# Wide token-major projections and a first unit moved forward, in a hybrid decoder block on one core

## The reference

```python
mg = h @ w_in[:, gate columns]                            # 2 x 1024 columns, "mg"
b_ssm = y_ssm @ w_branch_ssm                              # "bs"
b_nsa = o_nsa @ w_branch_nsa                              # "bn"
merged = sigmoid(mg[:, :1024]) * b_ssm + sigmoid(mg[:, 1024:]) * b_nsa
x = x + merged @ w_out                                    # "wo"
a = clamped_swiglu(t @ w_gate_up[e] + b_gate_up[e])       # per expert e
out = out + combine[:, e:e + 1] * (a @ w_down[e] + b_down[e])
```

## Time and profile before

| | |
|---|---|
| runs | 1303.49 median, 1302.44 to 1305.95 (n = 3) |
| profiled execution | 1304.99 us, span 1303.3 |
| granted clock, mean | 0.992 |
| PE busy | 1222.0 us, 94% of the span |
| DVE, ACT, POOL busy | 444.3, 281.1, 105.4 us |
| DMA | 454.08 MB, mean 348 GB/s |
| chain that ended last | PE 58%, DMA 31%, DVE 6%, ACT 3% |
| its largest lines | weights of w_gate_up 28%, PE L1032 20%, PE L1046 10%, PE L749 5% |

### The profile page before, as it was taken

How to read it: one execution, slowest core, us unless ns; L and a number is a source line. 1 busy time by engine, 2 the same in 40 slices (tenths; PEclk the granted TensorE clock), 3 DMA queues, 4 the chain that set the end, 5 groups by cost and what they waited for, 6 DMA issues and landing times.

```text
span 1303.3 us, 17482 instructions
## 1 busy us (share of the span) xinstructions
PE 1222.0 (94%) x7089; PEld 654.2 (50%) x7089; DVE 444.3 (34%) x914; ACT 281.1 (22%) x507; POOL 105.4 (8%) x89
## 2 busy tenths in 40 slices
PE   6999998999889999999999989898989999898985
PEld 6999987899853343343333324232323323242321
DVE  6866566665533222222122212122122212122113
ACT  4673437662321000110011101010101101010101
POOL 1301301453500000000000000000000000000000
PEclk9989999999989999999999999999999999999999
DMA  7647433225989999999999999999999999999994
GB/s 225 210 129 227 130 103 124 98 98 161 367 351 367 426 428 428 428 428 430 428 428 428 430 427 428 428 430 427 428 428 429 428 427 429 429 428 428 427 428 210
DMA packets 79964, 454.08 MB, mean 348 GB/s; under 512 B 10160, under 2 KB 53296, under 8 KB 55344
## 3 DMA queue, kind: packets, MB, share of 16 engines
q1 hardware_dynamic: 76960, 451.30, 84.8%
q10 hardware_dynamic: 2960, 2.17, 0.6%
HBM read 452.40 MB, written 1.05 MB: 348 GB/s over the span
## 4 chain that ended last, share of the span: by engine, by line
PE 58%; DMA 31%; DVE 6%; ACT 3%; issue 1%; ACTq 1%; POOL 0%; DVEq 0%; SPq 0%
DMA ring<-in_w_gate_up_dram 28%; PE psum L1032 20%; PE psum L1046 10%; PE psum L746 9%; PE psum L749 5%; PE psum L1021 5%; PE psum L1072 3%; DMA ring<-in_w_down_dram 3%; PE psum L700 2%; DVE WL L1461 2%; ACT WH L1173 1%; PE psum L956 1%; PE psum L1003 1%; PE psum L827 1%; DMA PR<-in_cmp_pos_v_dram 1%
## 5 line engine op out<-in xcount | busy, mean ns | idle before, releaser
L1032 PE MATMUL psum<-ring,ZS 128*64 128x512 f32 x1504 | 355.3, 616 | 13.6 <-DMA ring<-in_w_gate_up_dram 13.5
L1032 PEld LDWEIGHTS psum<-ring,ZS 128*64 128x64 f32 x1504 | 100.0, 134 | 229.7 <-issue 192.4
L1894 DVE TENSOR_TENSOR X<-X,psum 128x1024 f32<-128x1024 f32 x64 | 75.3, 1218 | 387.8 <-PE psum L1072 387.8
L1046 PE MATMUL psum<-ring,HT 128*64 128x512 f32 x784 | 176.3, 596 | 20.4 <-DMA ring<-in_w_down_dram 19.7
L1878 DVE TENSOR_SCALAR ZS<-psum 128x512 f32<-128x512 f32 x32 | 22.1, 692 | 316.3 <-PE psum L1032 316.3
L1032 PE MATMUL psum<-slot,ZS 128*64 128x512 f32 x528 | 123.8, 615 | 2.0 <-DMA slot<-in_w_gate_up_dram 2.0
L1046 PEld LDWEIGHTS psum<-ring,HT 128*64 128x64 f32 x784 | 54.5, 136 | 129.6 <-issue 104.6
L1461 DVE TENSOR_TENSOR WL<-ring,WH 128x2048 fp32r<-128x2048 f32 (+1 forms) x42 | 98.4, 2344 | 56.7 <-ACT WH L1173 56.7
L1380 ACT ACTIVATE HT<-psum 128x512 f32<-128x512 f32 x32 | 19.1, 597 | 324.3 <-PE psum L700 324.3
L1173 ACT ACTIVATE WH<-ring 128x2048 fp32r<-128x2048 f32 (+1 forms) x42 | 78.5, 1874 | 13.1 <-PE psum L749 9.3
L1032 PEld LDWEIGHTS psum<-slot,ZS 128*64 128x64 f32 x528 | 35.7, 134 | 73.3 <-issue 64.6
(11 more groups left out here) (321 smaller groups left out, 1230.1 us busy)
## 6 DMA issues: line engine op xcount, KB each, us to landing
ring<-in_w_gate_up_dram SPq DMA_DIRECT2D x94, 2048.0 KB, 33.8
ring<-in_w_down_dram SPq DMA_DIRECT2D x49, 2048.0 KB, 35.1
slot<-in_w_gate_up_dram SPq DMA_DIRECT2D x33, 2048.0 KB, 33.8
ring<-in_w_in_dram SPq DMA_DIRECT2D x30, 1024.0 KB, 5.5
slot<-in_w_down_dram SPq DMA_DIRECT2D x15, 2048.0 KB, 35.0
ring<-in_w_branch_ssm_dram SPq DMA_DIRECT2D x4, 1024.0 KB, 4.9
ring<-in_w_branch_nsa_dram SPq DMA_DIRECT2D x4, 1024.0 KB, 4.9
ring<-in_w_out_dram SPq DMA_DIRECT2D x4, 1024.0 KB, 4.9
```

What stands on the lines that cost most here:

```text
L1032: ins = mm(psum[64 * (c % 2):64 * (c % 2) + 64, c // 2, :], XTS[:, k, s], every_other_pair(w[:, 2048 * (k % 2):2048 * (k % 2) + 2048], c), ...
L1046: ins = mm(psum[64 * h:64 * h + 64, 2, :], lhs, w[:, at:at + 512], start=(j + hf + k == 0), stop=(j == 1 and hf + k == 2))
L1894: v.tensor_tensor(xo, xo, psum[:, 3 + 2 * t:5 + 2 * t, :], ALU.add).then_inc(o_read, 1)
```

## The change

Units of mg, bs, bn and the first two of wo are cut the other way: 512 rows of weights by 512 columns. Two neighbouring units make a pair: the even one does the first half of the contraction, the odd one the second, into the same banks. A pair holds two banks, one per token half, and is evicted after its odd unit: t = 0 at H, t = 1 at P. A half of a unit is 3 passes of 4 matmuls with 512 columns. bn's halves wait only for the PV results that they read, so bn 0 and bn 1 join the list of fillers; the steps 0, 1 and 2 take two halves each. W now stands ahead of its H. MT and the first XX work by token half (four blocks of one t) rather than by column pairs. wo 2 and wo 3 stay as they were.

```diff
@@ order of the tokens
-    for x in [("mg", m) for m in range(2, 8)] + [("bs", m) for m in range(4)]:
+    for x in [("mg", m) for m in range(2, 8)] + [("bs", m) for m in range(4)] + [("bn", 0), ("bn", 1)]:
         halves += [("H", u[x]), ("P", u[x])]
...
         out.append(halves.pop(0))
+        if k < 3:
+            out.append(halves.pop(0))
...
     out += halves + [("LD", 0)]
-    for m in range(4):
-        unit("bn", m)
-        if m >= 1:
-            out.append(("MT", m - 1))
-    out.append(("MT", 3))
...
+    for m, behind_h, behind_p in ((2, [("MT", 0)], [("MT", 1)]), (3, [], [])):
+        out += [("H", u[("bn", m)]), *behind_h, ("P", u[("bn", m)]), *behind_p]
+    out += [("H", u[("wo", 0)]), ("MT", 2), ("P", u[("wo", 0)]), ("MT", 3)]
+    out += [("H", u[("wo", 1)]), ("P", u[("wo", 1)]), ("XX", 0)]
+    out += [("H", u[("wo", 2)]), ("RM", 0), ("XX", 1), ("P", u[("wo", 2)]), ("RM", 1)]
+    out += [("H", u[("wo", 3)]), ("XX", 2), ("P", u[("wo", 3)]), ("RM", 2)]
@@ loads on SP
+                    if wide(u):
+                        rows = slice(512 * (m % 2), 512 * (m % 2) + 512)
+                        c0 = first.get(kind, 0) + 512 * (m // 2)
+                        sp.dma_start(slot_view(u, 4, 512), w[0, rows, c0:c0 + 512].rearrange("(k p) n -> p k n", p=P)
+                                     ).then_inc(full, 16)
@@ PE
+            def wide_half_unit(u, t):
+                kind, m = UNITS[u]
+                h = m % 2
+                b, before = bank_of[u][t], freed[u][t]
+                if h == 0:
+                    pe.wait_ge(proj_free[b], before)
+                if kind == "bs" and m == 0 and t == 0:
+                    pe.wait_ge(ys_ready, 1)
+                if kind == "bn":
+                    pe.wait_ge(pv_read, 8 * t + 4 * h + 4)
+                if kind == "wo":
+                    pe.wait_ge(mt_ready, 2 * h + t + 1)
...
+                for n, (w, src) in enumerate([(wh, high), (wh, low), (wl, high)]):
...
+                    if n == 1 and kind == "wo":
+                        pe.wait_ge(mt_low, 2 * h + t + 1)
+                    for k in range(4):
+                        ins = mm(bank(b, 512), src[:, 4 * h + k, P * t:P * t + P], w[:, k, :],
+                                 start=(h == 0 and n == 0 and k == 0), stop=(h == 1 and n == 2 and k == 3))
+                if t == 1:
+                    ins.then_inc(unit_done, 1)
+                elif h == 1:
+                    ins.then_inc(wide_half, 1)
@@ DVE, eviction of bn
+                        ga = GA[:, t, D + 512 * q:D + 512 * q + 512]
+                        v.scalar_tensor_tensor(out=ga, in0=ga, scalar=1.0, in1=psum[:, b],
+                                               op0=ALU.add, op1=ALU.mult).then_inc(proj_free[b], 1)
+                        dve.wait_ge(proj_free[b], freed[k][t] + 1)
+                        v.tensor_tensor(MG[:, t, cols], MG[:, t, cols], ga, ALU.add).then_inc(mg_ready, 1)
```

More of the change, by code:

```diff
@@ L76, with wide @@
 SPLIT_UNITS = [u for u, (kind, _) in enumerate(UNITS) if kind not in ("w1k", "w1v")]
+def wide(u):
+    kind, m = UNITS[u]
+    return kind in ("mg", "bs", "bn") or (kind == "wo" and m < 2)
+PAIRS = [u for u in range(NU) if wide(u) and UNITS[u][1] % 2]
 def token_order():
@@ L165, in token_order @@
                 low.append(("L", SPLIT_UNITS[i]))
+        order.append(token)
+        if token[0] == "RW":
+            order += low
+            low = []
         if not first <= n < last:
@@ L392, in hybrid_block @@
                 continue
-            bank_of[u], freed[u] = n % 3, uses[n % 3]
-            uses[n % 3] += 1
-            n += 1
+            if wide(u) and UNITS[u][1] % 2:
+                bank_of[u], freed[u] = bank_of[u - 1], freed[u - 1]
+                continue
+            took = []
+            for _ in range(T if wide(u) else 1):
+                took.append((n % 3, uses[n % 3]))
+                uses[n % 3] += 1
+                n += 1
+            bank_of[u], freed[u] = zip(*took) if wide(u) else took[0]
         def slot_view(u, *dims):
@@ L712, in _ @@
             pe.wait_ge(const_done, 2)
+            def wide_half_unit(u, t):
+                kind, m = UNITS[u]
+                h = m % 2
[8 more added lines that the diff above has]
+                    pe.wait_ge(mt_ready, 2 * h + t + 1)
+                high, low = {"bs": (YSH, YSL), "bn": (OTH, OTL), "wo": (HTH, MTL)}.get(kind, (HTH, HTL))
+                i = SPLIT_UNITS.index(u)
+                wh, wl = part(WH[i % SPLITS], 0, 4, 512), part(WL[i % SPLITS], 0, 4, 512)
+                if t == 0:
+                    pe.wait_ge(wh_ready, i + 1)
+                for n, (w, src) in enumerate([(wh, high), (wh, low), (wl, high)]):
+                    if w is wl and t == 0:
+                        low_ready(pe, i)
+                    if n == 1 and kind == "wo":
[7 more added lines that the diff above has]
+                    ins.then_inc(wide_half, 1)
             def half_unit(u, half):
                 kind, m = UNITS[u]
+                if wide(u):
+                    return wide_half_unit(u, half)
                 b = bank_of[u]
@@ L720, in half_unit @@
                         pe.wait_ge(proj_free[b], freed[u])
[L721 to L724, removed]
                 feature_major = kind in ("xbc", "kc", "vc", "ks", "kw", "q", "z")
-                high, low = {"bs": (YSH, YSL), "bn": (OTH, OTL), "wo": (HTH, MTL)}.get(kind, (HTH, HTL))
+                high, low = (HTH, MTL) if kind == "wo" else (HTH, HTL)
                 rows = slice(P * half, P * half + P)
@@ L964, in _ @@
                         pe.wait_ge(mt_low, k - 1)
[L965 to L968 removed]
+                    q, t = k // 2, k % 2
+                    for j in range(4):
+                        ins = tr(bank(3 + k % 2, 4, P)[:, j], MG[:, t, P * (4 * q + j):P * (4 * q + j) + P])
                     ins.then_inc(mt_full, 1)
@@ L982, in _ @@
                     pe.wait_ge(h2t_act, k + 1)
-                    for t in range(T):
-                        router(k, t)
+                    if k < 2:
+                        for m in range(2):
+                            router(m, k)
+                    else:
+                        for t in range(T):
+                            router(2, t)
             for t in range(T):
```

137 lines of the change are left out of this document (76 added, 61 removed).

## The result

The changed kernel takes **1289.79 us** (median of four runs, 1288.22 to 1291.53) against 1302.97 (four runs, 1301.91 to 1305.95) of the kernel before on the same chip: a ratio of 0.9898, 95% interval 0.9881 to 0.9915, or 13.2 us faster. The prediction was 1288.3, inside 1282 to 1296. Two later sets of runs of the same kernel, each on its own chip, gave 1290.24 and 1289.70, with 1304.60 and 1304.35 for the kernel before beside them: 14.4 and 14.7 us between the medians, 13.7 and 13.4 by the ratios.

The account below looks back on a forecast made before the run. The expert weight stream was taken as the bound, its end set by the dense stage's end: 1304.99 less 15.2 gives 1289.8, and the median 1.5 below that 1288.3, range 1282 to 1296 us.

Parts of the forecast that it names:

- The last unit: Last half unit before the expert part: ends 15.2 us earlier than 363.47, at 348.3.
- Width: Half units: 512-column matmuls at 218 ns, bounds 213 and 248; a half takes 2.7 us with re-entry instead of 2.98.
- Steps 0 to 4: Early attention: three more half units done, PT5 at 240.0 instead of 237.74, so 2.3 us later.
- Steps 5 to 16: Later attention: ACT/DVE loop at 12.1 us per two steps; 0.8 gained where PE was bound; PV15 ends at 304.1.
- The tail to wo 1: PV15 to wo1's end: ten halves, four transpose groups, 1.4 us wait on DVE; ends 333.7, 15.6 earlier.
- The clock: Tail: the 0.73 granted clock behind the 3.71 us pause cost 1.6 us; the share should now be near one.
- The weights: Expert loads: shift 12.4 (first two), 10.5 (third), 13 (fourth), 15 to 16 us (others); stream ends 15.2 earlier.
- (a): Whole dense stage: PE is the only bound, contention mild; 19 to 21 us earlier, 1284; chance 0.17.
- (b): Tail: DVE low parts at 4.23 beside POOL and the clock falls again; 10 us earlier, 1293.5; chance 0.13.
- (c): Expert weight stream: queue full from the third load, so only its 10.5 us shift counts; 1293; chance 0.06.
- (d): Split-format 512-column matmul takes about 427 ns, decisive from 274; some 66 us slower, 1370; chance 0.03.
- (e): No difference: moved halves push the loop by the tail's saving, halves no shorter (248 ns), PV15 at 312 or later; chance 0.03.

Follow-up runs that it names:

- The experiment on the width: Changed kernel with every 512-column matmul split into two of 256 columns: 1293.12 us, 2.9 above the changed kernel on the same chip.
- the order experiment: Changed kernel with MT 2 and MT 3 both ahead of wo 0's halves: 1296.25 us, 6.0 above the changed kernel.
- the experiment with the third load: Changed kernel with the third expert load issued behind wo 0 instead of behind bn 3: 1291.03 us, 0.8 above the changed kernel on the same chip.
- the kernel with nothing moved: Changed kernel with wide units and reordered tail kept, but no half unit moved into the attention: 1296.10 us, 5.9 above the changed kernel.

## Why the prediction was right, and where its terms were not

**The whole.** Mechanism and size held: a forecast gain of 15.2 us, 13.3 in the trace's stretch, 13.2 in the medians (14.4 and 14.7 on the two other chips). That the profiled executions differ by 15.9 is no confirmation, since 2.0 of it are ahead of the change. The last unit was to end 167.4 us behind the start of the stretch (348.3 less 180.92) and ended at 169.24, 1.9 late. Of that, 0.7 had come by the end of PV(15) and 1.2 came in the tail up to wo 1. The terms, all counted from that start:

- **Width.** I took 218 ns from the nearest row, 215 ns; it is 227, 213 for the columns and 13.5 more. With bounds of 213 and 248 it is inside, and a half unit is 2.72 back to back, and 2.86 behind anything else, where I had 2.62 and 2.7. This is the mis-sized term; of the signs that the prediction named, the spacing of 215 to 220 ns and the last unit at 348 (350.2 in the same count) are the ones that did not come. The rule quoted in the prediction (the Trainium skill, "TensorE: Matmul & The Clock Gate", section Back-to-back issue gap, about 131 ns) is contradicted by the operation itself now.
- **Steps 0 to 4.** The times came nearly to the tenth: the bank of mg 4's second half at 33.67 (33.6 forecast), PT(2) at 44.13 (44.0), PT(4) at 53.82 (54.0), the SSM output's low part at 56.37 (56.3), PT(5) at 59.14 (59.1), with the wait on VectorE's copy that the forecast named. But two errors cancel here, which is luck. Between 33.67 and 53.82 five half units took 14.2 us (2.90, 5.58, 2.87, 2.86) where 13.5 were forecast, and three groups of transposes, PV and scores took 1.98 each where 2.3 were forecast. The timeline of before has 2.01 for such a group, from PT(1) at 214.90 to the half unit at 216.91.
- **Steps 5 to 16.** From PT(5) to the end of PV(15) 64.1 were forecast and 64.75 came. Before it was 64.87, so the 0.8 us that this part was to gain came to 0.1: the six steps from PT(9) to PT(15) gained 0.66 (34.73 against 35.39), and the steps from PT(5) to PT(9) took 0.54 back (23.03 against 22.49). The mechanism was only half right: I had the ACT and DVE loop as the bound at 12.1 us for two steps; the steps run at 2 x 6.13 = 12.26 with no listed wait of PE behind 261.09 and up to 301, so PE is the bound, with the loop just behind. The experiment on the width shows both: the pitch follows PE's width to 6.25, in full from PT(9) on, and still only 1.3 of some 3.4 us of width count in all up to PV(15).
- **The tail to wo 1.** Forecast 29.6, measured 30.81. Four groups of transposes took 1.4 (1.6 forecast) and the wait 1.19 (1.4). Ten halves with their re-entries took 28.2, not 26.6: 1.0 for the width (27.2 at 2.72 each where 26.2 were forecast) and 0.6 for the re-entries, which cost 1.0, not 0.4. The wait was right by two errors that cancel. ScalarE was not held up as forecast: the DMA issues ran from 303.55 beside the split, and wo 0's high part was ready at 311.0, which is 1.6 earlier than forecast in the same count. VectorE so had pauses that I had denied it (1.68 and 1.45 us), and then paid more for its low parts, 3.12 twice, where I had 2.5.
- **The clock.** The fall to 0.73 is gone with the pause; the order experiment brings both back together.
- **The weights.** The first two loads moved by 13.2 and the next five by 10.8, 11.2 and 8.8 without the 2.0 (12.4 and 10.5 forecast for the first and the third). It doesn't matter, as the experiment with the third load shows: the time behind the last half unit is 938.4 to 941.2 us in all twelve profiles of this study, the kernel before included.

**The rivals.** (a) PE as the only bound was right on who is the bound in the steps, wrong in its sum, because it counted the width at 0.28 per half. (b) Contention of 4.23 per low part with a fall of the clock did not occur, though the kernel with nothing moved has 4.2 us low parts and a wait of 2.24. (c), (d) and (e) are out: third load, 227 ns where (d) decides from 274, PV(15) at 304.8 in the count of before where (e) needs 312. The 14 us of pauses in the sum of (d) are more than the rows give: the listed waits of PE from 181 to 349 add up to 10.6 and the clock behind the last of them cost 1.6.

**Where the gain lies.** Undone one at a time, the three parts cost 2.7 (width), 5.9 (halves moved into the attention) and 4.7 (order of the tail) us of stretch. That they add up to the 13.3 of the whole is partly luck, since each of these kernels has its own wait in wo 1.

## What to carry to other kernels

Work that fits beside a chain that another engine bounds is worth its time less what the chain then slips: here a half unit of 2.7 us costs 1.1 in the early steps and 0.7 in a late one, so look for work to fill both ends of such a loop, not only the end with the visible pauses. An independent operation between a producer and the transposes that wait for it pays twice where the clock falls behind the pause, as it did behind 3.71 and 4.47 us here and not behind 1.19 or 2.24. And compare two profiles from the first changed instruction on, since they can differ by microseconds before it.

## What the hardware showed that I had not expected

- A matmul in this split format costs its columns at 2.4 GHz and some 13.4 ns more at the two widths compared: 227 ns at 512 (213.3 + 13.5), 120 at 256 (106.7 + 13.3). Doubling the width so saves 13 ns per pair, 6%. It does not go on downwards: eight matmuls of 64 columns take 0.89 us (62.33 to 63.22), 112 ns each.
- A VectorE operation with two SBUF operands that starts while a GpSimd instruction runs ends as if it had started when that instruction ended. Timeline of POOL, after:

```profile
319.16 1.38 POOL L689 CAST BG<-KD 32x1024 bf16<-32x1024 f32 x1
320.63 4.06 POOL L691 TENSOR_TENSOR BG<-KD,BG 32x1024 bf16<-32x1024 f32 x1
324.75 1.38 POOL L683 CAST BG<-YV 96x1024 bf16<-96x1024 f32 x1
```

  The three are two casts and a subtraction. The low part of 319.57 ends at 322.69, 2.15 behind the cast's end of 320.54, where it takes 2.29 by itself; the sum of 323.32 ends at 325.23, 0.54 behind 324.69 (0.69 by itself); the low part of 325.16 ends at 328.28, 2.15 behind 326.13. The operation of 322.61, with one operand in PSUM, takes 0.68 as always. The trace agrees with the Trainium skill, "SBUF — State Buffer", section SBUF: two separate sides, by which the engine that comes second to the shared ports waits out the other's whole instruction. What this costs a VectorE operation is then bounded by the rest of one GpSimd instruction, and is not a factor on VectorE's time. It holds in every case between 300 and 345 us of the twelve profiles: 43 low parts end 2.14 or 2.15 behind the GpSimd instruction, the 4.23 us ones included, and 27 sums 0.54 to 0.56 behind it. GpSimd pays too: its subtraction of line 685 takes 2.15 us at 315.86 and 4.07 at 326.21.
- The clock falls in the dense stage vary in depth between executions of the same kernel (granted 0.91, 1.00 and 0.91 over 60 to 80 us in three executions of the changed kernel, 0.83 in the kernel before), and move everything behind them: 0.83 over 20 us is 3.4 us.
